# Hybrid decoder block: compression chunks interleaved with projection chunks, and a rearranged opening

## The reference

```python
h = rmsnorm(x, norm1_w)                     # x: (1, 256, 1024)
proj = h @ w_in                             # columns: gq gk gv gz | ga gb | nq | kc vc ks vs kw vw | ngate | mgate
y_a = gated_deltanet(gq, gk, gv, gz, ga, gb, ...)       # 8 heads of 128, causal conv, chunked delta rule
y_b = native_sparse_attention(nq, nkv, ngate, ...)      # compressed, selected and window branches
x = x + (sigmoid(gate_a) * (y_a @ w_proj_a) + sigmoid(gate_b) * (y_b @ w_proj_b)) @ w_out
h2 = rmsnorm(x, norm2_w)
x = x + (silu(h2 @ w_gate) * (h2 @ w_up)) @ w_down
```

## Time and profile before

| | us |
|---|---|
| median of three executions (670.12 to 671.31) | 670.36 |
| the profiled execution | 671.74 |
| its span, first to last instruction | 669.6 |
| PE busy | 615.3 |
| DVE busy | 375.4 |
| ACT busy | 288.2 |
| POOL busy | 35.9 |

### The profile page before, as it was taken

The page is one execution under the profiler, slowest core; times in us unless marked ns, Lnnn a source line. Parts: engine busy times, 40 slices in busy tenths (PEclk is TensorE's granted clock), DMA queues, the critical chain, the costliest instruction groups (busy, mean ns, idle before and its releaser), DMA issues.

```text
span 669.6 us, 11335 instructions
## 1 busy us (share of the span) xinstructions
PE 615.3 (92%) x4696; PEld 579.9 (87%) x4696; DVE 375.4 (56%) x619; ACT 288.2 (43%) x475; POOL 35.9 (5%) x54
## 2 busy tenths in 40 slices
PE   0999998896899988899989999999699999999996
PEld 0789998875898888898979999999699999999995
DVE  1669888765715343655665546565555554455553
ACT  3366564113324334743545454434543334334441
POOL 2100000222500000300000000000000000000000
PEclk9999999897899789997989999999799999999999
DMA  9555554129343341344125345547366666666631
GB/s 270 157 148 182 156 160 136 55 65 324 98 129 88 102 133 62 121 127 127 64 63 189 99 155 188 176 142 192 79 190 185 186 180 188 190 185 187 189 126 63
DMA packets 110459, 98.00 MB, mean 146 GB/s; under 512 B 4690, under 2 KB 106127, under 8 KB 110410
## 3 DMA queue, kind: packets, MB, share of 16 engines
q1 hardware_dynamic: 105904, 93.40, 45.5%
q0 software_dynamic: 1632, 2.47, 1.7%
q10 hardware_dynamic: 2874, 1.44, 0.8%
HBM read 96.52 MB, written 1.45 MB: 146 GB/s over the span
## 4 chain that ended last, share of the span: by engine, by line
PE 81%; DVE 9%; ACT 5%; DMA 2%; issue 1%; ACTq 1%; POOL 1%; DVEq 0%; POOLq 0%
PE ps L1151 21%; PE ps L1152 21%; PE ps L1153 20%; PE ps L1271 4%; PE ps L1156 4%; DVE w_lo L754 2%; ACT w_hi L480 2%; PE ps L1412 2%; PE ps L1305 2%; PE ps L1387 2%; PE ps L1258 1%; PE ps L1223 1%; PE ps L1409 1%; DMA sub_m<-sub_a 1%; DMA sub_a<-AXb 1%
## 5 line engine op out<-in xcount | busy, mean ns | idle before, releaser
L754 DVE TENSOR_TENSOR w_lo<-raw,w_hi 128x2048 fp32r<-128x2048 f32 x79 | 181.1, 2292 | 150.8 <-ACT w_hi L480 150.7
L1151 PE MATMUL ps<-h_hi,w_hi 128*128 128x256 f32 x832 | 241.9, 291 | 6.0 <-issue 6.0
L1152 PE MATMUL ps<-h_lo,w_hi 128*128 128x256 f32 x832 | 238.2, 286 | 0.0
L1153 PE MATMUL ps<-h_hi,w_lo 128*128 128x256 f32 x832 | 238.0, 286 | 0.0
L480 ACT ACTIVATE w_hi<-raw 128x2048 fp32r<-128x2048 f32 x79 | 150.7, 1908 | 67.8 <-PE ps L1153 63.6
L1151 PEld LDWEIGHTS ps<-h_hi,w_hi 128*128 128x128 f32 x832 | 162.6, 195 | 7.7 <-issue 7.2
L1152 PEld LDWEIGHTS ps<-h_lo,w_hi 128*128 128x128 f32 x832 | 162.7, 196 | 0.6 <-issue 0.2
L1153 PEld LDWEIGHTS ps<-h_hi,w_lo 128*128 128x128 f32 x832 | 162.4, 195 | 0.0
L566 ACT ACTIVATE sg<-ps 128x256 f32<-128x256 f32 x22 | 8.4, 383 | 75.0 <-PE ps L1153 75.0
L664 ACT ACTIVATE sc<-sc,s_nm 128x128 f32<-128x128 f32 (+1 forms) x32 | 14.3, 448 | 47.1 <-DVE s_nm L1016 47.1
L1151 PE MATMUL ps<-w_hi,g_hi 128*128 128x512 f32 x88 | 34.4, 390 | 0.0
(11 more groups left out here) (322 smaller groups left out, 961.0 us busy)
## 6 DMA issues: line engine op xcount, KB each, us to landing
raw<-in_w_in SPq DMA_DIRECT2D x34, 1024.0 KB, 5.3
raw<-in_w_gate SPq DMA_DIRECT2D x22, 512.0 KB, 4.0
raw<-in_w_up SPq DMA_DIRECT2D x22, 512.0 KB, 5.2
raw<-in_w_down SPq DMA_DIRECT2D x11, 1024.0 KB, 5.0
raw<-in_cmp_w SPq DMA_DIRECT2D x8, 1024.0 KB, 5.5
raw<-in_w_proj_a SPq DMA_DIRECT2D x4, 1024.0 KB, 5.3
raw<-in_w_proj_b SPq DMA_DIRECT2D x4, 1024.0 KB, 5.2
raw<-in_w_out SPq DMA_DIRECT2D x4, 1024.0 KB, 5.1
```

The source lines that it names most:

```text
L754: nc.vector.tensor_tensor(w_lo[s % NSPL][:], raw[n % NRAW][:], w_hi[s % NSPL][:].bitcast(f32), ALU.subtract).then_inc(lo_done, 1)
L1151: pe.matmul(bank, lhs(lh), rhs(rh), start=start, stop=False)
L1152: pe.matmul(bank, lhs(lh), rhs(rl), start=False, stop=False)
L1153: return pe.matmul(bank, lhs(ll), rhs(rh), start=False, stop=stop)
```

## The change

1. **Chunk order.** After kc and vc come nq 0, cmpk 0, nq 1, cmpk 1, nq 2, cmpk 2, nq 3, cmpk 3, ks, cmpv 0, kw, cmpv 1, cmpv 2, vs, cmpv 3, vw. The same chunks as before; slots 12, 13 and everything from gz 0 (slot 30) keep their numbers.
2. **Stages and small products.** `SOLVE_GAP` goes from 13 to 18 half slots and `SOLVE_AFTER` from 5 to 6, so that `X4` moves from the second half of slot 22 to the first of slot 25, and `o1` from slot 28 to the second half of slot 30. W2_K, TURN_KC, TURN_KS, LOGITS_C, TURN_KW, the four TURN_PC and W2_V stand in slots 23 to 30; TURN_PC+3 and W2_V share the second half of slot 30 with `o1`.
3. **Opening.** Four of ACT's transfers move to SP, behind chunks 1 and 2. ACT runs a one-column Exp ahead of x. The two squares of x run on ACT and DVE at once, and so do the two normalisations. Chunk 0 is split in halves: ACT makes both high halves ahead of `h_hi`, DVE the first low half, POOL the second. PE starts chunk 0 without the narrow columns.
4. **Moved small work.** The narrow columns' split goes to slot 2, their products to slot 3, `small_gates` to slot 4, the decay factors to slot 6, the bias table's products to slot 2 (copied in slot 3).

```diff
-    out += [("kc", 0), ("vc", 0)] + [("cmpk", i) for i in range(4)] + [("nq", i) for i in range(4)]
-    out += [("ks", 0)] + [("cmpv", i) for i in range(4)] + [("vs", 0), ("kw", 0), ("vw", 0)] + [("gz", i) for i in range(4)]
+    out += [("kc", 0), ("vc", 0)]
+    for i in range(4):
+        out += [("nq", i), ("cmpk", i)]
+    out += [("ks", 0), ("cmpv", 0), ("kw", 0), ("cmpv", 1), ("cmpv", 2), ("vs", 0), ("cmpv", 3), ("vw", 0)] + [("gz", i) for i in range(4)]
...
-BEFORE_SOLVE, SOLVE_AFTER, SOLVE_GAP = len(STAGES), 5, 13
+BEFORE_SOLVE, SOLVE_AFTER, SOLVE_GAP = len(STAGES), 6, 18
...
+W2_K, TURN_KC, TURN_KS, LOGITS_C, TURN_KW, TURN_PC, W2_V = 0, 1, 2, 3, 4, 5, 9
+MISC_SLOTS = {W2_K: (AT["cmpv", 0], 1), TURN_KC: (AT["kw", 0], 1), TURN_KS: (AT["cmpv", 1], 0), LOGITS_C: (AT["cmpv", 1], 1),
...
+            load_chunk(1)
+            sp.dma_start(upper[:], c_upper).then_inc(const_in, 16)
+            sp.dma_start(negmask[:], c_negmask).then_inc(const_in, 16)
+            load_chunk(2)
...
+            pool.wait_ge(hi_done, 1)
+            nc.gpsimd.tensor_tensor(w_lo[0][:, KT // 2:, :], raw[0][:, KT // 2:, :], w_hi[0][:, KT // 2:, :].bitcast(f32),
+                                    ALU.subtract).then_inc(first_lo, 1)
...
+            act.wait_ge(ones_set, 1)
+            nc.scalar.activation(warm[:], ones[:, 0:1], ACT.Exp)
             act.wait_ge(x_in, 16)
-            for t in range(TT):
-                nc.scalar.activation(xn_sb[:, t, :], x_sb[:, t, :], ACT.Square, accum_out=scol["x"][:, t:t + 1]).then_inc(xss, 1)
-            split_hi(0)
...
+            nc.scalar.activation(xn_sb[:, 0, :], x_sb[:, 0, :], ACT.Square, accum_out=scol["x"][:, 0:1]).then_inc(xss, 1)
+            act.wait_ge(rstd_ready, 1)
+            nc.scalar.activation(xn_sb[:, 1, :], x_sb[:, 1, :], ACT.Copy, scale=scol["x"][:, 5:6]).then_inc(xn_done, 1)
+            act.wait_ge(raw_in[0], 16)
+            nc.scalar.activation(w_hi[0][:, 0:KT // 2, :], raw[0][:, 0:KT // 2, :], ACT.Copy).then_inc(first_hi, 1)
+            nc.scalar.activation(w_hi[0][:, KT // 2:, :], raw[0][:, KT // 2:, :], ACT.Copy).then_inc(hi_done, 1)
...
-                    small_gates()
...
-                if n == 1:
-                    decay_factors()
...
+                if n == 2:
+                    small_split()
+                if n == 3:
+                    small_out()
+                if n == 4:
+                    small_gates()
+                if n == 6:
+                    decay_factors()
...
+            dve.wait_ge(x_in, 16)
+            nc.vector.tensor_tensor_reduce(xn_sb[:, 1, :], x_sb[:, 1, :], x_sb[:, 1, :], 1.0, 0.0, ALU.mult, ALU.add,
+                                           accum_out=scol["x"][:, 1:2]).then_inc(xss, 1)
...
+                    if n == 3 and half == 0:
+                        small_columns()
```

More of the change, by code:

```diff
@@ L121, in slot_solves @@
     return 2 * (n - FIRST_STAGE_SLOT) + half == BEFORE_SOLVE + SOLVE_AFTER
[L127 to L131, removed]
+W2_K, TURN_KC, TURN_KS, LOGITS_C, TURN_KW, TURN_PC, W2_V = 0, 1, 2, 3, 4, 5, 9
+MISC_SLOTS = {W2_K: (AT["cmpv", 0], 1), TURN_KC: (AT["kw", 0], 1), TURN_KS: (AT["cmpv", 1], 0), LOGITS_C: (AT["cmpv", 1], 1),
+              TURN_KW: (AT["vs", 0], 0),
+              TURN_PC: (AT["vw", 0], 0), TURN_PC + 1: (AT["vw", 0], 1), TURN_PC + 2: (AT["gz", 0], 0), TURN_PC + 3: (AT["gz", 0], 1),
+              W2_V: (AT["gz", 0], 1)}
 def slot_misc(n, half):
@@ L260, in hybrid_block @@
         zw = own("zw", [P, 1])
+        warm = own("warm", [P, 1])
         scol = {n: own("s_" + n, [P, 8]) for n in ("c", "d", "x", "nm", "se", "fac")}
@@ L715, in _ @@
                 for half in range(2):
+                    if n - 1 in (AT["cmpk", 3], AT["cmpv", 3]) and half == 0:
+                        act.wait_ge(half_done, 2 * n)
+                        nc.scalar.activation(hid_tok[:], ps[6][:, 0:CW], ACT.Copy).then_inc(hid_raw, 1)
                     for name in slot_stages(n, half):
                         gdn(name)
[L718 to L724 removed]
+                    if n - 1 in (AT["cmpk", 3], AT["cmpv", 3]) and half == 1:
+                        hidden(0 if n - 1 == AT["cmpk", 3] else 1)
                     for m in slot_misc(n, half):
@@ L1174, in _, with small_columns @@
             pe.matmul(ps[6][0:HEADS, 0:384], relb[:], onehot[:], start=True, stop=True).then_inc(pre_pe, 1)
-            pe.wait_ge(pre_act, 1)
-            pe.wait_ge(pre_dve, 3)
-            for k in range(KT):
-                pe.wait_ge(h_hi_done, k + 1)
-                pe.wait_ge(h_lo_done, k + 1)
-                last = three(((wsm_hi, wsm_lo), (h_hi, h_lo)), ps[1][0:NSMALL, 0:SEQ],
-                             lambda a: a[:, k, :], lambda a: a[:, k, :], k == 0, k == KT - 1)
-            last.then_inc(pre_pe, 1)
+            def small_columns():
+                pe.wait_ge(pre_act, 1)
+                pe.wait_ge(pre_dve, 4)
+                for k in range(KT):
+                    last = three(((wsm_hi, wsm_lo), (h_hi, h_lo)), ps[7][0:NSMALL, 0:SEQ],
+                                 lambda a: a[:, k, :], lambda a: a[:, k, :], k == 0, k == KT - 1)
+                last.then_inc(pre_pe, 1)
             def decay_columns():
@@ L1419, in _ @@
                     last.then_inc(half_done, 1)
-                    if n == 0 and half == 0:
+                    if n == 3 and half == 0:
+                        small_columns()
+                    if n == 3 and half == 1:
                         pe.wait_ge(small_raw, 1)
@@ L1424, in _ @@
                         last.then_inc(small_mm, 1)
-                    if n == 1 and half == 1:
+                    if n == 6 and half == 0:
                         decay_columns()
+                    if n == 2 and half == 1:
                         pe.wait_ge(bias_in, 32)
```

82 lines of the change are left out of this document (44 added, 38 removed).

## The result

The changed kernel is **slower by 1.5%**: 680.21 us median of four executions (679.08 to 682.55) against 670.84 of the kernel before on the same chip (670.12 to 671.60), ratio 1.0153 with a 95% interval of 1.0125 to 1.0181. The forecast was 680.2. In a second comparison the same kernel came to 681.29 against 668.61, ratio 1.0197 (1.0159 to 1.0235). Of the 0.4% between the two ratios the larger part lies in the kernel before, whose median was 670.84 in the first comparison and 668.6 to 669.3 in the four others; so "slower by 1.5 to 2%" is what can be said. One execution of `squares_last` (experiment 4), of 3321.25 us, is in the slow state and left out; all others compared are in the fast one.

A forecast was written before the change was run, and what follows sets the result against it. PE was busy 615.3 of 669.6 us, so only its waits, lower clock and work could move the time. Opening -6.7, slot 4 +4.5 and new order +12.0 gave +9.8: 681.5 profiled, 680.2 median, range 671 to 688.

The forecast's parts named there:

- The new order: Reordered chunks, stages and small products: 32.6 us of waits and clock added, 20.6 removed, +12.0 in sum.
- the removed ones: Six waits at the old places from 108 to 287 us, 6.0 at nq 0 the longest: 15.4 us gone.
- The chain of the forecast: Between full chunks, the next split follows the last evacuation on ACT: 5.7 us, of which PE covers 2.1.
- The clock: PE runs at a lower clock after a wait: 1.5 us for each new wait over 3, bounds 0 and 2.1.
- the terms, 6.0 for four places less 5.2: Clock prices of 1.5 us at nq 2, nq 3, ks and kw, less three old low stretches that go.
- the 1.5 for W2_V: Clock price behind W2_V's wait of 4.5 us in slot 30, 6.0 together.
- The opening: Start of the kernel: PE starts chunk 0 near 16.3 instead of the narrow columns at 23.00, -6.7 us.
- Slot 4: `small_gates` in a slot of 6.65 us makes PE wait 3.0 at chunk 6, plus 1.5 of clock: +4.5.
- The faster case: High splits run ahead of evacuations, so four waits and their clock vanish (21.0 us): 660.7; chance 0.08.
- The reordering does nothing for loads: Compression chunks still wait for their loads: 686 if four come 1.5 us late each; chance 0.03.

The follow-up runs named there:

- squares_last: The changed kernel with the sixteen squares of `o1` put behind the copies of the last transposed pc and W2_V in ACT's program: 677.88 us, ratio 1.0127.
- experiment 12: The changed kernel itself, with nothing altered, executed once more: 681.29 us.
- experiment 3: The changed kernel with ACT's high split ahead of the evacuation in the four slots of a lone compression chunk: 664.66 us, ratio 0.9920.
- experiments 4 and 6: 4 is `squares_last`; 6 is the changed kernel with `o1`'s squares in fours behind units 0 to 3, DVE's norm behind unit 4: 676.87 us, ratio 1.0100.
- new_order: The kernel before with only the changed kernel's order of chunks, stages and small products, over the old opening: 681.74 us, ratio 1.0183.
- gates_early: The changed kernel with the narrow columns, their transposes and `small_gates` one to two slots earlier: 676.69 us, ratio 1.0106.

## Why the prediction came out right

**Bounds.** The reading that only waits and PE's pace could move held: PE runs the same 4696 instructions, and DVE's and ACT's busy times are within 0.6 of those before. The pace, though, has a part that the granted clock does not show (experiment 12).

**The new order** was forecast at +12.0 and took +12.6 in the profile, +12.3 in the medians (1.83% of 669). Its waits one by one, forecast and measured: nq 2, nq 3 and ks 3.6 each, 3.2 each on the split and 0.3 before it on the square, together 3.5; kw 4.2, 4.4; `m1t` 1.5, 1.6; kc 2.3, 1.8; `T4` behind LOGITS_C 1.8, 2.0; W2_V 4.5, 4.5. (Three of the forecast's sums are 0.1 or less off their own terms: 9.5 - 7.3 is 2.2, not 2.3; W2_V's 1.3 + 4.7 + 0.6 is 6.6; slot 4's chain is 16.3.) The sum is 25.1 against 24.9, and the removed ones all went as named (15.4 forecast, 15.6 gone).

**The mechanism** of the largest of these, ACT's program order, is shown by experiment 3: it alone takes away 12.6 of the 14.0 and the clock with it. The chain of the forecast (copy, square, high split, low split, 5.7) took 184.2 to 189.8, 5.6. For W2_V experiments 4 and 6 show the block of squares as the cause: the wait of 4.5 is 0.7 in both. What I had not seen is that DVE's program has the norm of the same block in it.

**The clock** was the term that was mis-sized, in both directions. The price of 1.5 for a wait over 3 was 2.3 at nq 2, nq 3 and ks and 1.5 to 1.7 at kw and gz 1 (and 1.4 to 1.6 at nq 2 and nq 3 in `new_order` and `gates_early`); behind the wait of 2.4 at chunk 6 it was nothing in the first execution and 1.4 in the second. In kc to gz 1 PE's busy time rose by 3.5, where the terms, 6.0 for four places less 5.2, give 0.8; the 1.5 for W2_V, which falls behind gz 1's start, was paid there and made up inside the units, so that stretch is 0 where the forecast has 1.5. The +2.7 has a source that the forecast put at nothing: behind the wait of 1.8 on kc the clock is low from 215 to 219 (0.50 from 216 to 218), which costs 1.7. Some 0.8 each at nq 2, nq 3 and ks comes on top, and LOGITS_C, which stood in a low stretch of 3.4 before (221 to 229), now stands in one of 1.5 (228 to 232). The two misses, +2.7 and -1.5, work against each other, and so the sum is still within 1 of the forecast. That a wait of 2.2 had no low stretch in the earlier trace rows was read as a bound between waits; experiment 12 says that the same wait may or may not have one.

**The opening**, forecast -6.7, moved PE's first product from 23.00 to 15.94, 7.1; counted from the 21.92 at which `new_order` reached the same product, it is 5.8 to 6.0 (16.10 and 15.94 in the changed kernel's two executions). Its chain in the changed kernel: squares to 7.4, small instructions to 9.8, ACT's half normalised to 11.0, then PE; POOL's half:

```profile
13.29 2.54 POOL L434 TENSOR_TENSOR w_lo<-raw,w_hi 128x1024 fp32r<-128x1024 f32 x1 [7.76 <-ACT w_hi L507]
```

POOL took 2.54 where 2.3 were worked out from the earlier trace rows, and in this execution PE's start followed its end by 0.11, as forecast. One sentence of that step was wrong: that PE's slow pace after its rest lasts as long either way. It depends on the execution (experiment 12). The rule of the Trainium skill (SBUF — State Buffer, Who interferes with whom), by which DVE's row with two SBUF inputs and POOL's reading block each other, is neither borne out nor refuted by these rows: POOL's row starts 0.34 before DVE's first low half ends (12.40 and 1.23), DVE took as long without POOL beside it, and POOL's row is 0.27 longer than the estimate of 2.27, which a block up to DVE's end would explain as well as a slower instruction.

**Slot 4** was forecast at +4.5, a wait of 3.0 and 1.5 of clock. Measured: 2.4, and 0 or 1.4. The chain on ACT and DVE:

```profile
54.51 0.21 ACT L525 ACTIVATE c_t<-c_t 128x16 f32<-128x16 f32 x1 [2.52 <-DVE c_t L848]
54.75 1.28 ACT L526 ACT_TABLE_LOAD   x1
56.04 0.31 ACT L526 ACTIVATE c_t<-c_t,ones 128x16 f32<-128x16 f32 x1
56.37 1.28 ACT L528 ACT_TABLE_LOAD   x1
...
58.02 1.90 ACT L496 ACTIVATE w_hi<-raw 128x2048 fp32r<-128x2048 f32 x1
```

It ran from DVE's start at 53.62 to the low split's end at 62.31 as worked out, 15.8 after the start of chunk 4 instead of 16.35. The table loads are 1.28 again, with 0.03 around them: the 2.7 of the Trainium skill (ScalarE: Activation LUTs, Rules for kernel authors) would have made the wait 5.2 or more, and it was 2.4.

**The rivals.** The faster case hung on high splits that run ahead of the evacuations. They do not in this kernel, and experiment 3 ran the kernel in which they do: 664.7, where the rival said 660.7. "The reordering does nothing for loads" is refuted, PE waits for no landing in the changed kernel; it is what bounds experiment 3. The mechanism and the waits were right; that the medians hit 680.2 to a tenth is luck on top: the two profiles of the changed kernel lie 7.3 and 9.7 above the one before, and the two ratios differ by 0.4%.

## What to carry to other kernels

These are lessons from one kernel. Between two chunks that need a split, interleaving a cheap one is only worth something if the split's instruction stands ahead of whatever waits for the chunk that is still running: an engine that runs its program in order makes a short slot as long as its whole chain (evacuate 1.2, split high 1.9, split low 2.3). Before moving a block of work on one engine, look for the instruction on the other engines that waits for its end and at what is queued behind that one. And read an expected gain off several executions: parts of a trace that belong to the execution (PE's slow start, a low stretch behind a wait of 2.4) were here as large as the opening's whole net gain.

## What was unexpected of the hardware

- PE's slow start is not in the granted clock: 17 products in 3.56 us and 31 in 3.53 are both given as 1.00. The 17 start 0.21 apart, as the products do in the rows at 0.50. With transposes from 11.0 and 11.1 on, PE reached its fast pace before 16.1 in one execution of the changed kernel and at 19.7 in the other, 1.6 us of time. The Trainium skill (TensorE: Matmul & The Clock Gate, Part 1) says that the number of slow matmuls at the start differs from run to run; the traces agree.
- A wait of 2.4 was followed by a low stretch in one execution of the same kernel and by none in another, and waits of 3.19 cost 1.4 to 2.3 in the half chunk behind them, by the trace.
- POOL's subtraction of 1024 columns took 2.54 us, and DVE's of the same size 1.23, with POOL's beside it for its last 0.34, against 1.22 alone.
